# HGRN2 mixer on one Trainium2 core: forward and backward masked scores summed before one product with the values

## What is computed

```
def gla_forward(q, k, v, log_f, s0):
    ...
    s_prev, _ = _inter_chunk_states(k_c, v_c, b_c, s0)
    o_inter = jnp.einsum('bhnck,bhnkv->bhncv', q_c * jnp.exp(b_c), s_prev)
    b_mid = b_c[:, :, :, CHUNK // 2 - 1:CHUNK // 2]
    a = jnp.einsum('bhnck,bhnsk->bhncs', q_c * jnp.exp(b_c - b_mid), k_c * jnp.exp(b_mid - b_c))
    a = jnp.where(jnp.tril(jnp.ones((CHUNK, CHUNK), dtype=bool)), a, 0.0)
    o_intra = jnp.einsum('bhncs,bhnsv->bhncv', a, v_c)
    return (o_inter + o_intra).reshape(b, h, t, -1)
...
    o_f = gla_forward(q, k_f, v, lf_f, s0_f)
    o_b = _rev(gla_forward(_rev(q), _rev(k_b), _rev(v), _rev(lf_b), s0_b))
    o = (o_f + o_b).transpose(0, 2, 1, 3)
```

## Time and profile before

| | us |
|---|---|
| median of 3 runs | 2196.77 |
| lowest and highest | 2195.98, 2197.83 |
| the profiled execution | 2198.93 |
| its span, first to last instruction | 2197.1 |

### The profile page before, as it was taken

How to read it: one execution, slowest core, us unless ns; L and a number is a source line. 1 busy time by engine, 2 the same in 40 slices (tenths; PEclk the granted TensorE clock), 3 DMA queues, 4 the chain that set the end, 5 groups by cost and what they waited for, 6 DMA issues and landing times.

```text
span 2197.1 us, 30841 instructions
## 1 busy us (share of the span) xinstructions
PE 2111.0 (96%) x11810; PEld 1526.6 (69%) x11810; DVE 1284.9 (58%) x2328; ACT 930.7 (42%) x1968; POOL 475.5 (22%) x441
## 2 busy tenths in 40 slices
PE   5899999999999999999999999899999999998998
PEld 2667767777777777777777777677666666665665
DVE  7847547547557547557457457655553536465444
ACT  5745345345355355355255355444423131214222
POOL 2021222222222322322313212000151312100110
PEclk8899999999999999999999999899999999999999
DMA  6210110110110110210110110534221110203443
GB/s 273 91 53 11 45 53 11 51 47 11 58 39 11 58 39 11 63 34 11 63 35 14 59 34 21 182 125 144 97 71 51 39 63 19 86 10 134 150 148 114
DMA packets 106746, 144.36 MB, mean 66 GB/s; under 512 B 7136, under 2 KB 74224, under 8 KB 105584
## 3 DMA queue, kind: packets, MB, share of 16 engines
q1 hardware_dynamic: 99648, 125.72, 17.6%
q10 hardware_dynamic: 6960, 16.80, 2.0%
HBM read 108.91 MB, written 33.57 MB: 65 GB/s over the span
## 4 chain that ended last, share of the span: by engine, by line
PE 83%; ACT 6%; DVE 6%; issue 2%; DMA 1%; SPq 0%; DVEq 0%; ACTq 0%
PE bank L1253 22%; PE bank L1254 22%; PE bank L1258 21%; PE bank L1408 3%; PE bank L1393 3%; PE bank L1388 3%; PE bank L1419 3%; PE bank L1508 3%; PE bank L1372 1%; DVE xa L1036 1%; ACT kp L713 1%; DMA ada_sb<-in_ada_w 1%; DVE lacc L1095 1%; ACT junk L385 1%; PE bank L1350 1%
## 5 line engine op out<-in xcount | busy, mean ns | idle before, releaser
L1253 PE MATMUL bank<-h_hi,w_hi 128*128 128x512 f32 (+1 forms) x1472 | 576.7, 397 | 0.0
L1254 PE MATMUL bank<-h_hi,w_lo 128*128 128x512 f32 (+1 forms) x1472 | 549.6, 378 | 0.0
L1258 PE MATMUL bank<-h_lo,w_bf 128*128 128x512 bf16 (+1 forms) x1472 | 328.6, 366 | 0.0
L1253 PEld LDWEIGHTS bank<-h_hi,w_hi 128*128 128x128 f32 x1472 | 278.9, 189 | 55.5
L1254 PEld LDWEIGHTS bank<-h_hi,w_lo 128*128 128x128 f32 x1472 | 279.1, 190 | 47.5
L1258 PEld LDWEIGHTS bank<-h_lo,w_bf 128*128 128x128 bf16 x1472 | 133.7, 98 | 142.7 <-issue 25.2
L1253 PE MATMUL bank<-wo_hi,og_hi 128*128 128x512 f32 x512 | 207.3, 405 | 11.9 <-DVE wo_lo L1128 7.8
L1066 DVE SCALAR_TENSOR_TENSOR w_st<-w_st,cv,bank 128x128 f32<-128x128 f32 x560 | 193.6, 346 | 30.0 <-PE bank L1408 6.2
L1254 PE MATMUL bank<-wo_hi,og_lo 128*128 128x512 f32 x512 | 202.2, 395 | 0.0
L578 POOL TENSOR_TENSOR q<-qp,cv 128x512 f32<-128x512 f32 x64 | 78.8, 1231 | 541.0 <-PE bank L1393 273.4
L553 POOL TENSOR_TENSOR w_hi<-w_raw,zero_col 128x512 fp32r<-128x512 f32 x80 | 91.9, 1149 | 425.9 <-PE bank L1258 224.3
(11 more groups left out here) (168 smaller groups left out, 3533.8 us busy)
## 6 DMA issues: line engine op xcount, KB each, us to landing
w_raw<-in_w_in SPq DMA_DIRECT2D x80, 256.0 KB, 2.7
ada_sb<-in_ada_w SPq DMA_DIRECT2D x8, 1024.0 KB, 13.7
xt<-in_x SPq DMA_DIRECT2D x16, 512.0 KB, 6.0
ada_a<-in_ada_late SPq DMA_DIRECT2D x64, 128.0 KB, 2.0
ada_b<-in_ada_late SPq DMA_DIRECT2D x64, 128.0 KB, 2.1
gated_scratch<-o_t ACTq DMA_DIRECT2D x32, 256.0 KB, 2.4
og<-gated_scratch SPq DMA_DIRECT2D x16, 512.0 KB, 4.1
xr<-in_x SPq DMA_DIRECT2D x16, 512.0 KB, 4.9
```

The costliest lines, as they stand in the source:

```text
L1253: pe.matmul(out_ap, hi, m_hi, start=start, stop=False)
L1254: pe.matmul(out_ap, lo, m_hi, start=False, stop=False)
L1258: return pe.matmul(out_ap, bf, m_lo, start=False, stop=stop)
```

## The change

It makes the forward intra-chunk products go away. `am` has four buffers, one for each block. The forward masked scores stay in them. The backward ones go to a new tile `am_b`. VectorE adds the two into `asum` (a new instruction in steps 18 to 21, ahead of the state chain), and only the backward output product multiplies with `v_tok`, taking `asum`. In the forward groups the output is the inter-chunk product alone, and `o_done` is raised behind it.

To have room for the tiles, the two buffers and the sum of the late pieces move onto `k_tok`, with waits on SP and ACT for that, and `grow` moves onto a weight buffer, with a wait on ACT behind the last head. The late pieces of the first head move: three a step in steps 5 to 8 and four in step 9, where there were two a step from step 4 on. Their sums on PE move from steps 8 and 12 to 7 and 10 (first head: from 11 and 14 to 9 and 10).

```
-def late_index(st, first, top):
-
-    i = 2 * (st - (4 if first else 1)) - (1 if top else 0)
-    return i if 0 <= i < NLATE else None
+def late_pieces(st, first, top):
+
+    if first:
+        n = 4 if st == 9 else 3
+        seen = range(3 * (st - 5), 3 * (st - 5) + n) if 5 <= st <= 9 else range(0)
+        return seen[:1] if top else seen[1:]
+    i = 2 * (st - 1) - (1 if top else 0)
+    return range(i, i + 1) if 0 <= i < NLATE else range(0)
...
-    return {11: 0, 14: 1}.get(st) if first else {8: 0, 12: 1}.get(st)
+    return {9: 0, 10: 1}.get(st) if first else {7: 0, 10: 1}.get(st)
...
+                            if i == 0:
+                                need(sp, "u_done", NF, h, 0)
...
+                        if fi == 0:
+                            need(act, "late_acc", NLATE, h, NLATE)
+                        if fi == 1:
+                            need(act, "late_mm", 2, h, 2)
...
+            act.wait_ge(s["gate_out"], 16)
...
+                    if 6 <= fi < NF:
+                        ai = lat(fi)
+                        need(dve, "a_masked", NA, h, ai + 1)
+                        need(dve, "o_done", NA, h, ai)
+                        dve.tensor_tensor(asum[:, :, :], am[:, GROUPS[F0 + fi][1], :, :], am_b[:, :, :], ALU.add
+                                          ).then_inc(s["a_summed"], 1)
...
-                        dve.copy_predicated(am[:, 2 * d + ai % 2, :, :],
+                        if d == 1:
+                            need(dve, "a_summed", 4, h, ai - 4)
+                        dve.copy_predicated(am[:, ai, :, :] if d == 0 else am_b[:, :, :],
...
-                            pe.matmul(o[r, c // 2 * P:(c // 2 + 1) * P], q2[:, ai % 2, c * CHUNK:(c + 1) * CHUNK],
-                                      w_st[:, (8 * ai + n) % 16, :], start=(n < 2), stop=False,
-                                      skip_group_check=True)
-                        need(pe, "a_masked", NA, h, ai + 1)
-                        for j in range(4):
-                            last = pe.matmul(o[:, j * P:(j + 1) * P], am[:, 2 * d + ai % 2, j, :],
-                                             v_tok[:, 2 + 4 * b + j, :], start=False, stop=True,
+                            last = pe.matmul(o[r, c // 2 * P:(c // 2 + 1) * P],
+                                             q2[:, ai % 2, c * CHUNK:(c + 1) * CHUNK],
+                                             w_st[:, (8 * ai + n) % 16, :], start=(n < 2), stop=(d == 0),
                                              skip_group_check=True)
+                        if d == 1:
+                            need(pe, "a_summed", 4, h, ai - 3)
+                            for j in range(4):
+                                last = pe.matmul(o[:, j * P:(j + 1) * P], asum[:, j, :], v_tok[:, 2 + 4 * b + j, :],
+                                                 start=False, stop=True, skip_group_check=True)
                         last.then_inc(s["o_done"], 1)
```

More of the change, by code:

```diff
@@ L164, in hybrid_kernel @@
         extra_at = cursor[0]
-        lacc = place("lacc", [P, 2, LCOL], FP32)
-        ada1_b = place("ada1_b", [P, LCOL], FP32)
+        asum = place("asum", [P, 4, P], FP32)
+        junkh = place("junkh", [P, 2, P], BF16)
+        hss = place("hss", [P, 4], FP32)
+        hrs = place("hrs", [P, 4], FP32)
+        em = place("em", [P, 8], FP32)
+        cv = place("cv", [P, NF, 8], FP32)
+        assert cursor[0] <= extra_at + 6 * P * 4
         cursor[0] = extra_at + 6 * P * 4
@@ L177, in hybrid_kernel @@
         q2 = place("q2", [P, 2, BLK], FP32)
+        k_tok_at = cursor[0]
         k_tok = place("k_tok", [P, 2, 4, P], FP32)
@@ L181, in hybrid_kernel @@
         start_end = cursor[0]
[L182 to L185, removed]
         ge = place("ge", [P, NF, 9], FP32)
[L187 to L192, removed]
+        am_b = place("am_b", [P, 4, P], FP32)
+        cursor[0] = k_tok_at
+        ada1 = (place("ada1_a", [P, LCOL], FP32), place("ada1_b", [P, LCOL], FP32))
+        lacc = place("lacc", [P, 2, LCOL], FP32)
+        cursor[0] = after_h
         grow = place("grow", [4 * KT, P], FP32)
-        assert cursor[0] <= late_end
         cursor[0] = kp_at
@@ L288, in hybrid_kernel @@
                     k_ready lf_ready scanned centred e1_ready e_ready gates_x small x_done kt_tr kt_ready a_done
-                    a_masked u_done w_step q2_ready o_done o_read sq_ready o_tr rs_ln rs_ready og_mul og_ready
+                    a_masked a_summed u_done w_step q2_ready o_done o_read sq_ready o_tr rs_ln rs_ready og_mul og_ready
                     late_acc late_mm late_sum late_tr late_row gate_out gate_in mrow_zero ohi_ready olo_ready obf_ready
@@ L450, in head @@
                             load_x0(sp, t)
-                    for i in (late_index(st, first, False), late_index(st + 1, first, True)):
-                        if i is not None:
+                    for top in (False, True):
+                        for i in late_pieces(st + top, first, top):
+                            if i == 0 and first:
+                                sp.wait_ge(s["hf_ready"], KT * len(GT0))
+                            if i == 0:
+                                need(sp, "u_done", NF, h, 0)
                             load_late(h, i)
@@ L569, in head @@
                             pool.memset(am[:, i, :, :], 0.0).then_inc(s["zero_done"], 1)
+                        pool.memset(am_b[:, :, :], 0.0).then_inc(s["zero_done"], 1)
                     fi = st - (F0 + 2)
@@ L951, in head @@
                     if first and st == F0:
-                        dve.wait_ge(s["zero_done"], 4)
-                    late_piece(h, late_index(st, first, True))
+                        dve.wait_ge(s["zero_done"], 5)
+                    late_piece(h, late_pieces(st, first, True))
                     if st == LATE_ADD:
@@ L1080, in head, with late_piece @@
                         gate_out(h, st - (F0 + 11))
[L1081 to L1096, removed]
+                    late_piece(h, late_pieces(st, first, False))
+            def late_piece(h, pieces):
+                for i in pieces:
+                    k, half = i % KT, i // KT
+                    need(dve, f"late_in{i % 2}", 8 * NLATE, h, 16 * (i // 2 + 1))
+                    if k == 0:
+                        need(dve, "late_mm", 2, h, half - 1)
+                        dve.tensor_scalar(lacc[:, half, :], ada1[i % 2][:, :], head_tab[:, k, 4:5], None, ALU.mult
+                                          ).then_inc(s["late_acc"], 1)
+                    else:
+                        need(dve, "late_acc", NLATE, h, i)
+                        dve.scalar_tensor_tensor(lacc[:, half, :], ada1[i % 2][:, :], head_tab[:, k, 4:5],
+                                                 lacc[:, half, :], ALU.mult, ALU.add).then_inc(s["late_acc"], 1)
             def normalise_out(h, bi):
```

2 lines of the change are left out of this document (1 added, 1 removed).

## The result

The changed kernel takes 2209.76 us (median of 5 runs, 2206.84 to 2210.77) where the kernel before takes 2196.77 (5 runs, 2195.97 to 2197.83). The ratio is 1.0051, with a 95% interval of 1.0040 to 1.0062: slower by 13 us by the medians, by 11 by the ratio. The forecast was 2217 with 2193 to 2234, slower. The profiled executions show spans of 2207.9 and 2197.1 us.

What follows compares the result with a forecast made beforehand. PE and DVE were taken as near the bound together; collisions with POOL make seven heads 2.5 us later and the last 1.9, 19.4, plus 1 for the first head: profiled 2219.3, median 2217 us, range 2193 to 2234.

Steps and rivals of the forecast that it cites:

- What bounds: Steps 14 to 22 of a head: PE and DVE both within some 2 us of being the bound.
- The sum without collisions: One head without POOL stops: all but 0.15 of PE's 4.36 us lost to forward chains and the four sums.
- Collision 1: Step 14: POOL's earlier burst catches DVE one operation sooner, making the chain of g2 0.3 us later.
- Collision 2: Step 15: POOL's `q2` of g4 makes DVE's clamp wait 1.0 us; ACT and the scan are 0.7 later.
- Collision 3: Step 19: POOL's burst costs DVE 3.1 us instead of 0.85; the product of g7 goes 1.7 later.
- Collision 4: Steps 20 and 21: the clamp gets its 1.1 us back; the product of g9 is still 1.9 late.
- Collision 5: Step 22: POOL's next-head weights meet DVE's L1103, 1.0 us of waiting, 0.6 reaching PE; not in the last head.
- The first head: PE waits some 5 us for the sixteenth piece before step 10; net +1 us, ends -1 and +3.
- A: Rival: the collisions stay as they are, 8 x -0.15 + 1, 2197 us; chance 0.16.
- B: Rival: the moved bursts free DVE, 1.1 us a head won, 2189 us; chance 0.08.
- C: Rival: PE is the bound, so all 34.9 us come home, 2162 us; chance 0.04.
- D: Rival: the stops add up as DVE's lag feeds the next burst, 4.5 us a head, 2233 us; chance 0.14.

Runs made afterwards that it cites:

- the kernel without sums: Changed kernel with the four sums a head left out, backward product taking backward scores alone, forward intra-chunk part missing from the result: 2196.72 us, ratio 0.9997.
- the one with the products back: Changed kernel with the four forward intra-chunk products computed again on PE, their part counted twice in the result: 2208.20 us, ratio 1.0046.
- the kernel with both bursts moved: Changed kernel, first head's second late sum in step 11, POOL's z weights in step 16 (was 14), next v weights in 20 (was 19): 2182.25 us.

## Why the prediction was right, and where it was not

**What bounds.** Right, and the base of the rest. PE and DVE are near the bound together; PE waits 1.29 at g2 (forecast: all but 0.1 of step 14's 1.09, on top of the 0.18 of before) and 1.43 at g4. That the 34.9 us do not come home is shown twice, by the kernel without sums and by the one with the products back. Of the signs named in advance, the two waits and the stretched operations of step 19 are there; the clamp of 1.3 in step 15 is not, and the heads' period is 163.8, not 165.4.

**The sum without collisions** said 0.15 us a head ahead of before. The gain up to g6 measures 1.0 (7.19 at g1, 6.20 at g6), against the forecast 1.1.

**Collision 1** (step 14), 0.3: measured 0.03, the lateness of g2 against g1. The burst did start earlier and did stretch the clamp (1.13 for 0.29), as worked out. But from the clamp to the chain of g2 DVE needs no more than it did before, as it had met the rest of this burst there too, and so the product of g2 hardly moved.

**Collision 2** (step 15), 0.7 and the clamp held up for 1.0: **this step failed.** Clamp and `q2` do arrive together, and the clamp goes first, by 0.03 us:

```profile
520.77 0.42 DVE L1013 TENSOR_SCALAR xa<-xa 128x512 f32<-128x512 f32 x1
...
520.80 1.29 POOL L587 TENSOR_TENSOR q<-qp,cv 128x512 f32<-128x512 f32 x1 [2.27 <-PE bank L1409]
```

(DVE timeline, then POOL's.) `q2` waits instead, and the table L1019 behind it, which costs DVE 0.3 and nothing on the path that could be seen. My estimate had `q2` at 513.8 and the clamp at 513.85. With the 7.19 of the entry taken off, they came at 513.61 and 513.58: the 0.3 of collision 1 was missing, which shifts DVE's arrival more than POOL's. So this term stood on the one before, and on 0.05 us.

**Collision 3** (step 19) was the largest term, and it is there as described: L1019, L1025, L1033, L1041 and the sum are stretched, by about 0.4, 0.8, 0.4, 1.1 and 0.25 (rows of 0.61, 0.96, 1.09, 1.78 and 0.93), 3.0 us together, close to the forecast's 3.1. That it came out so near is in part luck. I had POOL 0.1 earlier and DVE 1.6 later; measured in the head, POOL is 1.0 earlier (557.60 against 551.41, with 7.19 at entry) and DVE 0.65 later, which moves them against each other by 1.65, where 1.7 was forecast. The errors of collisions 1 and 2 cancel here for the stops, but not for the time. The product of g7 loses 1.74 against that of g6, and lies 0.75 behind before (forecast 1.7). Moving the burst takes the 1.7 away.

**Collision 4** (step 20), the relief of the clamp (0.42 where it was 1.51): right. g9 lies 0.88 behind its lateness at entry, where 1.9 was forecast.

**Collision 5** (step 22), 0.6 a head: **this step failed too.** L1124 takes 0.81, and between g9 and the next entry a head loses 0.1 on average (-0.2 to 0.3). I had also overlooked that the burst already met this operation in the kernel before, where L1103 takes 0.94. It is there, with 1.66, in the kernel with the sum behind the chain, where DVE arrives 0.8 later against the burst, and with 1.63 in the kernel with both bursts moved. PE's waits before L1354 are then longer by 1.0 and 0.4 us a head. The mechanism exists; its size depends on where DVE stands.

**The first head** was put at +1 with -1 and +3 as ends. It was 4.7, with up to 2 us of scatter between profiles in it. The PE wait was right (5 forecast, 6.08 measured), and the wait of 2.43 in step 12, which should have hidden part of it, is indeed gone. (DVE took the sixteenth piece late for its own reason too: it waited 1.35 for the load of it, and 1.3 to 1.8 for the third piece of each step from 5 to 8. The kernel before has no such wait.) **What the sum left out** is the clock behind the wait. The granted clock was full (1.00) before the wait, and at 0.50 and 0.53, close to the lower of its two levels (1.2 GHz), in the two stretches of 3 us behind it (view of windows: stretch, us, PE, PEld, DVE, ACT and POOL busy, PEclk, DMA share, GB/s):

```profile
149.00:152.00 3.00, 2.86 (x9) 2.48 (x10) 1.48 (x7) 2.48 (x5) 0.00 (x0) 0.50 0.30 107
```

There the wide products start every 0.43 us, not every 0.23, and the projection of step 11 takes 7.7 us instead of 5.6: another 2.1. At the key transposes of step 11 PE is 9.3 late (157.74 against 148.41). Then 2.7 come back in step 12, where the kernel before has its 2.43 wait, and 1.7 in step 13, where that kernel has its own slow products behind the wait (0.43 us apart from 159.83 to 161.53). Of the later heads' rows none shows such products in either kernel.

So the sum of 19.4 + 1 was, measured by spans, about 6 (heads) + 4.7 (first head): the sign and the mechanism of step 19 right, a head at 0.99 where 2.5 was forecast, the first head at under a quarter of its price. The two errors partly cancelled, and that the time lies within the range owes something to this.

**Rivals.** A (nothing but 0.15) is out. B was said to depend on the clamp getting ahead of `q2`; it did, but step 19 still met the burst, so B's gain did not come. C is out by the kernel without sums: 2196.72, not 2162. D did not happen in the changed kernel; the kernel with the sum behind the chain is on the way to it.

What stays open: why the late pieces' new steps drift by 0.3 us a head when they stand alone and by 0.1 in the changed kernel, and where the up to 2 us come from by which the first entry differs between kernels with the same work ahead of it.

## What to carry to other kernels

When two engines run within a microsecond or two of each other, taking work off one is worth little until what holds up the other is taken away as well (here 0.8 of 4.36 us a head); look at both before either is edited, and test the pair, not each alone. Work on VectorE with its inputs in SBUF and work on GpSimd cost one another up to a whole operation where they met; here the bursts were cheapest under VectorE work that reads PSUM. A burst whose start hangs on a third engine moves when that engine's work is changed. The one-time parts (a first head, a single sum with a deadline) deserve a sum of their own: here one wait of 6 us in the first head made over a third of the loss, and the slower clock behind it was part of its price.

## What the runs showed of the hardware

The stops are between whole instructions and go either way. With POOL at work, DVE operations of 0.42 to 0.7 us took up to 1.8, and a copy of 8 elements a partition, 0.17 alone, took up to 1.04 (step 19 with the sum behind the chain). Operations that read PSUM next to SBUF, the chain steps among them, kept their time under the same bursts: eight chain steps took 3.11 under one (553.77 in the earlier trace rows) and 3.10 with POOL idle (518.40). Where both want to go on, they take turns: in the changed kernel's step 19 each POOL operation of the burst is followed by one or two of DVE's. And which goes first was settled by hundredths of a microsecond: the clamp, 0.02 to 0.03 us ahead of `q2` in the third to the eighth head, kept its length, and `q2` was stretched (1.29 for 1.04).

TensorE's granted clock fell from 1.00 to 0.50 within a wait of 6.08 us (first head of the changed kernel), and was back at 1.00 by 155 us; behind the wait of 2.43 in the kernel before, products were 0.43 us apart for 1.7 us. Behind the waits of up to 1.7 us in the later heads the products kept their 0.23.
